# S5 stage: three real products per complex product in the table fills, two more doublings on GpSimd, one fill and one state product moved ahead

## Chip, core and metric

The kernel runs on 1 core of one Trainium2 chip. The metric is the device time of one execution in microseconds, the median of several runs. Engines: TensorE (PE in the profile), VectorE (DVE), ScalarE (ACT), GpSimd (POOL) and the SyncE queue that starts the weight loads (SP).

## What is computed

A trunk of four layers over 256 tokens of width 1024. Each layer is a token mixer and a gated MLP, each behind an RMS norm. The mixer of layer 0 and 3 is sparse attention, of layer 1 RWKV-7, of layer 2 the S5 state space layer that the change is about:

```python
def s5_mixer(h, a_re, a_im, log_step, b_re, b_im, c_re, c_im, d_skip, w_glu, b_glu):
    step = jnp.exp(log_step.astype(f32))[:, None]
    lam = lax.complex(a_re, a_im)
    lam_bar = jnp.exp(lam * step)
    b_bar = ((lam_bar - 1.0) / lam)[..., None] * lax.complex(b_re, b_im)
    c = lax.complex(c_re, c_im)
    u = h as (256 tokens, 64 groups, 16 channels)
    bu = einsum('gpc,sbgc->sbgp', b_bar, u)          # 64 complex states per group
    states: x[t] = lam_bar * x[t-1] + bu[t]          # associative scan
    y = real(einsum('gcp,sbgp->sbgc', c, states)) + d_skip * h
    y = gelu(y); z1, z2 = split(y @ w_glu + b_glu)
    return z1 * sigmoid(z2)
```

## The kernel before

Each engine has its own program, written out by hand and ordered by semaphores. The weights of the MLP and of the GLU come in tiles of 1 MB. Each is split into a high and a low part: ScalarE rounds (L395, `w_high`), VectorE subtracts for half 0 of the tile and GpSimd for half 1 (L403, `w_low`), and TensorE multiplies with both parts (L420 to L422; in the down projection L788 and L790). Two tiles are held split at a time, so a split can begin when the tile two before it is used up.

The S5 mixer works in chunks of 8 steps. Its tables depend on the parameters alone, and are built while TensorE does the down projection of layer 1. `s5_tables(dve, part)` is called once behind each of the first `LAST_PART` = 11 of the twelve tiles of that projection, in `add_down`. Parts 5 to 7 build `coef`, the factors of the complex products. Part 8 begins a table of powers, `grid`, and doubles it from 1 to 4 entries; parts 9 and 10 double it to 8 and 16 on VectorE (`double(4)`, `double(8)`, L2591 to L2627). The last doubling, to 32 entries, is GpSimd's (`last_doubling`, L2333), and needs the end of part 10. The part numbers count 3 * m + g, and the last weight split of the projection is that of part 9's place; it stands in front of `double(4)`, and the addition of the last sums to `xT` (L639, `x_ready`) stands behind `double(8)`.

Then come eight fills. Fill f = 2q + lag writes one of two tables, FB (lag 0) or GC (lag 1), for quarter q. VectorE makes the four real products of a complex product, 128x1024 each (`products`, L2715), from the raw parameters and from factors that `coefs` copied to PSUM (L2724); GpSimd joins them pairwise in two additions (`s5_pool`, L2344, `fill_added`). Fill 0 is made before the norm of the layer (L514, L517), since it needs no activations. VectorE's order after the norm is fill 1, fill 2, turn and scan of states 0, fill 3, fill 4, turn and scan 1, fills 5 to 7, turn and scan 2, turn and scan 3. `turned_in(q)` and `scan(q)` (L2749 to L2775) need the products of TensorE's `states(q)` (L2514, `v_full`).

TensorE turns the activations (L2464, L2472), then works through, in order: turned tables 0 (L2487), states 0, lag table 0 (L2501), turned 1, states 1, lag 1, turned 2, lag 2, states 2, lag 3, turned 3, lag 4, states 3, lag 5, 6, 7, and at last `from_states` (L2539) and `from_inputs` (L2525). Turned tables q need fill 2q, lag tables 2q and 2q + 1 need fill 2q + 1. Lag tables 1 to 5 share banks, so each of them, and table 7, waits until ScalarE has masked the one before (L2389, 8 instructions). `from_states` needs the fourth scan (`x_state`).

Of the kernel before, what the change touches and what calls it, by code (L numbers as in the profile page):

```python
# [35 lines left out]
HALF = 64  # L36
# [152 lines left out]
def trunk(nc, A, out, layers=(0, 1, 2, 3)):  # L189
    plan = make_plan(layers)  # L190
    ctx = ExitStack()
    with ctx:
# [28 lines left out]
        half_pi = sb("half_pi", 1)  # L221
        eps = sb("eps", 3)
# [32 lines left out]
        def wait_full(eng, key, more=0):  # L255
# [8 lines left out]
                         q_scale=2, v_ready=4, qi_ready=2, ki_raw=3, ki_root=1, ki_ready=1,  # L264
# [581 lines left out]
        def mlp_pool(pool, L):  # L846
# [300 lines left out]
        def dsa_act(act, L):  # L1147
# [91 lines left out]
            act.activation(ki_rs, ki_sum, ACT.Sqrt, bias=eps[:, 0:1], scale=1.0 / HALF).then_inc(sem("ki_root"), 1)  # L1239
# [59 lines left out]
        def dsa_dve(dve, L):  # L1299
# [92 lines left out]
            dve.wait_ge(sem("ki_root"), 1 + since("ki_root", L))  # L1392
# [870 lines left out]
        coef = work[:, 14, 0:1024].rearrange("p (v k g) -> p v k g", v=4, k=S5_L)  # L2263
        grid_tmp = work[:, 14, 1024:1536]
# [17 lines left out]
        FB_RE, FB_IM, GC_RE, GC_IM = range(4)  # L2282
        S5_DMAS = (6, 4, 4)
        LAST_PART = 11
# [5 lines left out]
        near_coef = banks[6].rearrange("p (b v k g) -> p b v k g", b=2, v=4, k=S5_L)  # L2290
        turned_a, turned_b = (banks[i].rearrange("p (r z) -> p r z", r=2) for i in (2, 3))
        second_terms = [[work[:, s, a:a + 1024] for s, a in pair] for pair in (((14, 1024), (8, 1024)), ((18, 0), (18, 1024)))]
# [29 lines left out]
        def last_doubling(pool):  # L2322

            pool.wait_ge(sem("angles_ready"), 3)
            have = S5_N // 2
            factor = [small(x).unsqueeze(2).to_broadcast([P, S5_H, have]) for x in (L8_RE, L8_IM)]
            x = [x[:, :, 0:have] for x in grid]
            t = grid_tmp[:, 0:S5_H * have].rearrange("p (g n) -> p g n", n=have)
            for half in range(2):
                dst = grid[half][:, :, have:S5_N]  # L2330
                for out_, a, b, op in ((t, x[1], factor[1 - half], ALU.mult), (dst, x[0], factor[half], ALU.mult),
                                       (dst, dst, t, (ALU.subtract, ALU.add)[half])):
                    pool.wait_ge(pool_step.sem, pool_step.mark(pool.tensor_tensor(out_, a, b, op)))  # L2333
# [121 lines left out]
        def s5_pe(pe, L):  # L2455
# [102 lines left out]
            turned_tables(3)  # L2558
            lag_tables(4)
            states(3)  # L2560
# [46 lines left out]
        def s5_tables(dve, part):  # L2607
# [4 lines left out]
            def double(have):  # L2612
# [9 lines left out]
                if 2 * have < S5_N:  # L2622
                    tt(small(TMP), small(L8_IM), small(L8_IM), ALU.mult)
                    tt(small(TURNS), small(L8_RE), small(L8_RE), ALU.mult)
                    then(dve.scalar_tensor_tensor(out=small(L8_IM), in0=small(L8_RE), scalar=2.0, in1=small(L8_IM),
                                                  op0=ALU.mult, op1=ALU.mult))
                    ins = dve.tensor_tensor(small(L8_RE), small(TURNS), small(TMP), ALU.subtract)  # L2627
                    if 4 * have == S5_N:
                        ins.then_inc(sem("angles_ready"), 1)
                    else:  # L2630
                        then(ins)
# [42 lines left out]
            if part == 5:  # L2674
# [4 lines left out]
                then(dve.scalar_tensor_tensor(out=coef[:, GC_IM], in0=table(MAG_P, S5_L), scalar=-1.0, in1=table(U_IM, S5_L),  # L2679
# [490 lines left out]
```

## Time and profile before

| | |
|---|---|
| median of 3 runs | 1466.46 us (1465.0 to 1473.16) |
| profiled execution | 1465.52 us, its span 1463.8 us |
| mean granted TensorE clock | 0.991 of full |
| busy | PE 95%, DVE 70%, ACT 55%, POOL 43% |
| S5 tables on VectorE | 740.6 to 799.2 us of the span |
| S5 from its first product to the GLU | 800 to 885 us of the span |

The span is what the profiler saw between first and last instruction. A median over runs and the one profiled execution need not agree; steps below are read from the profiled one. The idle time of an engine counts only where the engine after it waits.

### The profile page before, as it was taken

What the parts mean: (1) busy time and instruction counts of PE and PEld (TensorE: products, weight loads), DVE (VectorE), ACT (ScalarE), POOL (GpSimd) and SP (SyncE); (2) the same over time, 40 slices, a digit from 0 to 9 for tenths busy, and PEclk for the clock granted to TensorE, in tenths of its full rate; (3) what the DMA queues carried; (4) which work ended last, traced back from release to release, by engine and by line L of the source; (5) the groups of instructions that cost most, each with busy time, mean ns of one, the idle gap of its engine ahead of it and who ended that gap; (6) DMA issues with size and microseconds to landing.
All of it is one profiled execution on the core that took longest, in us unless ns stands there. A gap on an engine that the chain in (4) does not pass through costs nothing.

```text
span 1463.8 us, 33117 instructions
## 1 busy us (share of the span) xinstructions
PE 1395.5 (95%) x13742; PEld 1315.6 (90%) x13742; DVE 1029.0 (70%) x1656; ACT 801.4 (55%) x1332; POOL 630.3 (43%) x341
## 2 busy tenths in 40 slices
PE   7999999999999888999999679999999999999998
PEld 7999999989887777999989579999989998999988
DVE  7675888733595555897779895888754776788842
ACT  5576666534651334665653346576654468576542
POOL 3343365541005202495554653365553332355553
PEclk9999999999999999999999889999999999999999
DMA  5643565562443001475554004555555552455553
GB/s 170 197 132 100 165 195 188 168 201 93 144 144 116 4 4 60 144 225 179 176 177 138 1 2 145 173 175 193 173 187 157 162 167 94 149 190 180 179 175 107
DMA packets 207895, 209.59 MB, mean 143 GB/s; under 512 B 7938, under 2 KB 206898, under 8 KB 207762
## 3 DMA queue, kind: packets, MB, share of 16 engines
q1 hardware_dynamic: 206624, 206.12, 43.7%
q0 software_dynamic: 800, 1.46, 0.6%
q8 instruction: 99, 1.62, 0.5%
q14 instruction: 34, 0.28, 0.1%
q10 hardware_dynamic: 338, 0.10, 0.0%
HBM read 206.62 MB, written 1.05 MB: 142 GB/s over the span
## 4 chain that ended last, share of the span: by engine, by line
PE 79%; DVE 13%; ACT 4%; issue 2%; DMA 0%; POOL 0%; ACTq 0%; SPq 0%; DVEq 0%
PE psum L420 17%; PE psum L422 17%; PE psum L421 17%; PE psum L788 7%; PE psum L580 5%; PE psum L790 3%; DVE work L2591 2%; DVE x_low L532 2%; DVE work L2715 1%; ACT w_high L395 1%; DVE work L517 1%; DVE w_low L403 1%; PE psum L1719 1%; PE psum L1733 1%; PE psum L1051 1%
## 5 line engine op out<-in xcount | busy, mean ns | idle before, releaser
L403 POOL TENSOR_TENSOR w_low<-ring,w_high 128x1024 fp32r<-128x1024 f32 (+1 forms) x185 | 458.2, 2477 | 676.0 <-ACT w_high L395 675.9
L420 PE MATMUL psum<-x_high,w_high 128*128 128x256 f32 x1728 | 491.0, 284 | 3.5 <-DVE w_low L403 1.4
L395 ACT ACTIVATE w_high<-ring 128x1024 fp32r<-128x1024 f32 (+1 forms) x368 | 376.4, 1037 | 213.8 <-PE psum L422 122.0
L422 PE MATMUL psum<-x_high,w_low 128*128 128x256 f32 x1728 | 489.0, 283 | 0.0
L421 PE MATMUL psum<-x_low,w_high 128*128 128x256 f32 x1728 | 488.9, 283 | 0.0
L403 DVE TENSOR_TENSOR w_low<-ring,w_high 128x1024 fp32r<-128x1024 f32 x183 | 295.2, 1613 | 172.9 <-ACT w_high L395 171.6
L420 PEld LDWEIGHTS psum<-x_high,w_high 128*128 128x128 f32 x1728 | 331.6, 192 | 5.9 <-issue 3.1
L421 PEld LDWEIGHTS psum<-x_low,w_high 128*128 128x128 f32 x1728 | 331.7, 192 | 0.0
L422 PEld LDWEIGHTS psum<-x_high,w_low 128*128 128x128 f32 x1728 | 331.6, 192 | 0.0
L788 PE MATMUL psum<-inner,w_high 128*128 128x512 f32 x528 | 187.0, 399 | 1.4 <-DVE w_low L403 1.4
L899 DVE SCALAR_TENSOR_TENSOR work<-psum,par,work 128x255 f32<-128x255 f32 (+1 forms) x352 | 144.6, 472 | 46.5 <-ACT work L820 46.3
L820 ACT ACTIVATE work<-psum,par 128x256 f32<-128x256 f32 x176 | 89.1, 559 | 131.3 <-PE psum L422 131.3
L790 PE MATMUL psum<-inner,w_low 128*128 128x256 f32 x528 | 148.1, 281 | 0.0
L788 PEld LDWEIGHTS psum<-inner,w_high 128*128 128x128 f32 x528 | 99.2, 188 | 26.6 <-DVE w_low L403 1.3
L790 PEld LDWEIGHTS psum<-inner,w_low 128*128 128x128 f32 x528 | 99.7, 189 | 0.0
L908 DVE TENSOR_TENSOR work<-work 128x512 f32<-128x512 f32 x44 | 81.2, 1844 | 6.9 <-DVE work L899 5.0
L580 PE MATMUL psum<-work,ring 128*128 128x256 f32 x384 | 84.2, 379 | 0.9 <-issue 0.9
L580 PEld LDWEIGHTS psum<-work,ring 128*128 128x128 f32 x384 | 72.8, 190 | 12.5 <-issue 2.9
L420 PE MATMUL psum<-w_high,x_high 128*128 128x256 f32 x256 | 75.2, 294 | 0.0
L849 POOL TENSOR_TENSOR inner<-work,inner 128x512 f32 (+1 forms) x44 | 74.7, 1702 | 0.0
L422 PE MATMUL psum<-w_high,x_low 128*128 128x256 f32 x256 | 72.4, 283 | 0.0
L421 PE MATMUL psum<-w_low,x_high 128*128 128x256 f32 x256 | 72.4, 283 | 0.0
(332 smaller groups left out, 2226.1 us busy)
## 6 DMA issues: line engine op xcount, KB each, us to landing
ring<-in_ffn_w_up_dram SPq DMA_DIRECT2D x88, 1024.0 KB, 5.1
ring<-in_ffn_w_down_dram SPq DMA_DIRECT2D x32, 1024.0 KB, 5.0
ring<-in_dsa_w_in_dram SPq DMA_DIRECT2D x28, 1024.0 KB, 5.3
ring<-in_ffn_w_down_dram SPq DMA_DIRECT2D x16, 768.0 KB, 4.3
ring<-in_rwkv_w_rkv_dram SPq DMA_DIRECT2D x12, 1024.0 KB, 5.0
ring<-in_dsa_w_out_dram SPq DMA_DIRECT2D x8, 1024.0 KB, 5.0
ring<-in_s_w_glu_dram SPq DMA_DIRECT2D x8, 1024.0 KB, 5.4
ring<-in_rwkv_w_out_dram SPq DMA_DIRECT2D x4, 1024.0 KB, 5.0
```

What stands on the lines that cost most here:

```text
L395: act.activation(high, raw, ACT.Copy).then_inc(sem("w_rounded", b), 1)
L403: eng.tensor_tensor(low, raw, high.bitcast(F32), ALU.subtract).then_inc(sem("w_split", b), 1)
L420: pe.matmul(out_, lhs[0], rhs[0], start=start, stop=False, skip_group_check=True)
L421: pe.matmul(out_, lhs[0], rhs[1], start=False, stop=False, skip_group_check=True)
L422: return pe.matmul(out_, lhs[1], rhs[0], start=False, stop=stop, skip_group_check=True)
L580: mm = pe.matmul(out_, parts[b][:, k, b * P:(b + 1) * P], x[:, k, :], start=start, stop=stop, skip_group_check=True)
L788: pe.matmul(banks[bank][:, :], high[:, k, :], inner[:, :, c, :], start=first, stop=False, skip_group_check=True)
L790: mm = pe.matmul(banks[bank][:, 0:T], low[:, k, :], inner_high[:, c, :], start=False, stop=last, skip_group_check=True)
L820: act.activation(conv[:, j % 3, h, b, :], bank_of(key)[:, b * T:(b + 1) * T], ACT.Identity, bias=col("ffn_conv_b", c + L * 2 * FC, r), sca ...
L849: pool.tensor_tensor(inner_low[:, at(2 * j, r), :], gated[:, j % 3], inner_high[:, at(2 * j, r), :].bitcast(F32), ALU.subtract).then_inc(s ...
L899: dve.scalar_tensor_tensor(out=row, in0=bank[:, b * T:(b + 1) * T - lag], scalar=col("ffn_conv_w", c + (L * 3 + tap) * 2 * FC, r), in1=row ...
L908: dve.tensor_tensor(gated[:, j % 3], conv[:, j % 3, 0], conv[:, j % 3, 1], ALU.mult).then_inc(sem("gated_done"), 1)
```

## The change

1. A complex product is made from three real products: with B = b_re + i b_im and factor x + i y, the fill takes (b_re + b_im) * x once, b_im * (x + y), and b_re * (y - x), and then one subtraction and one addition. So VectorE makes 3 products of 128x1024 per fill instead of 4; GpSimd still makes 2 additions. The sums of the raw parameters (`b_sum`, `c_difference`, new tiles of 128x512) are two new GpSimd instructions; VectorE's first product of fills 0 and 1 waits for them. The table of factors `coef` grows from four to six blocks, which costs two more instructions of 128x256 in part 5 and two in part 7, and makes the copy to PSUM 128x384; the copy is no longer double buffered.
2. `double(4)` and `double(8)` move from VectorE to GpSimd, behind GpSimd's last weight splits of the down projection. They wait for the end of part 8 on VectorE. Each has 6 instructions over the table and 5 over 128x32.
3. Fill 3 is made before turn 0 on VectorE, instead of behind scan 0.
4. `states(3)` comes before `lag_tables(4)` on TensorE.
5. In the attention layers the semaphore `ki_root` is folded into `ki_raw`; the same instruction counts up, and the same one waits.

```diff
         def mlp_pool(pool, L):
             for m in range(4):
                 for g in range(3):
                     ahead(rest_of_weights, pool, (L, "down", m, g), 1)
+                    if before_s5(L) and m == 3 and g < 2:
+                        doubling(pool, 4 * (g + 1))
...
-        LAST_PART = 11
+        LAST_PART = 9
...
+        def s5_raw_sums(pool):
+
+            pool.wait_ge(sem("s5_in", 2), 16 * S5_DMAS[2])
+            pool.tensor_tensor(b_sum[:, :, :], b_raw[:, 0], b_raw[:, 1], ALU.add).then_inc(sem("raw_sums"), 1)
+            pool.wait_ge(sem("c_ready"), 2)
+            pool.tensor_tensor(c_difference[:, :, :], c_raw[:, 0], c_raw[:, 1], ALU.subtract).then_inc(sem("raw_sums"), 1)
 
         def s5_pool(pool, L):
 
+            s5_raw_sums(pool)
             for f in range(FILLS):
                 q, lag = divmod(f, 2)
                 if f == 0:
-                    last_doubling(pool)
+                    doubling(pool, S5_N // 2)
                 for v in range(2):
                     out_ = (FB, GC)[lag][:, q, v].rearrange("p g z -> p (g z)")
-                    pool.wait_ge(sem("fill_products"), 4 * f + 2 * v + 2)
-                    pool.tensor_tensor(out_, out_, second_terms[1 - f % 2][v],
-                                       ALU.add if v != lag else ALU.subtract).then_inc(sem("fill_added"), 1)
+                    pool.wait_ge(sem("fill_products"), 3 * f + v + 2)
+                    pool.tensor_tensor(out_, shared_terms[f % 2], out_,
+                                       ALU.subtract if v == lag == 0 else ALU.add).then_inc(sem("fill_added"), 1)
...
+            states(3)
             lag_tables(4)
-            states(3)
...
         def products(dve, f):
-            if f == 1:
-                dve.wait_ge(sem("fill_added"), 1)
-            if f >= 2:
+            if f < 2:
+                dve.wait_ge(sem("raw_sums"), f + 1)
+            else:
                 dve.wait_ge(sem("fill_added"), 2 * (f - 1))
-            for out_, a, b in ((outs[0], re, x), (terms[0], im, y), (outs[1], re, y), (terms[1], im, x)):
-                dve.tensor_tensor(out_, a, b, ALU.mult).then_inc(sem("fill_products"), 1)
+            for out_, x, y in ((shared, both, real), (outs[0], im, total), (outs[1], re, difference)):
+                dve.tensor_tensor(out_, x, y, ALU.mult).then_inc(sem("fill_products"), 1)
...
             products(dve, 1)
             coefs(dve, 1)
             products(dve, 2)
+            products(dve, 3)
             turned_in(0)
             scan(0)
-            products(dve, 3)
             coefs(dve, 2)
             products(dve, 4)
```

Line numbers of the changed kernel are higher by a few; L2591 there is L2612, L2715 is L2739, L403 is L405. VectorE around the end of the projection, before: the last weight split (`w_low_53`), the two doublings, the last addition to `xT`, the copy of the factors and fill 0.

```order
L403 TENSOR_TENSOR w_low_53<-ring,w_high_51 128x768
L2591 TENSOR_TENSOR work<-work 128x128
L2591 TENSOR_TENSOR work<-work 128x32x4 x2
...
L2591 TENSOR_TENSOR work<-work 128x256
L2591 TENSOR_TENSOR work<-work 128x32x8 x2
...
L639 TENSOR_TENSOR xT<-xT,psum 128x512
L2724 COPY psum<-work 128x256
L2715 TENSOR_TENSOR work<-work,psum 128x1024 x4
L514 RECIPROCAL psum<-rstd 128x256
```

The same place now:

```order
L405 TENSOR_TENSOR w_low_53<-ring,w_high_51 128x768
L641 TENSOR_TENSOR xT<-xT,psum 128x512
L2748 COPY psum<-work 128x384
L2739 TENSOR_TENSOR work<-b_sum,psum 128x1024
L2739 TENSOR_TENSOR work<-work,psum 128x1024 x2
L516 RECIPROCAL psum<-rstd 128x256
```

Both doublings are gone from between the split and the addition, and fill 0 reads `b_sum`, which GpSimd writes. GpSimd at the same place now, from its last weight split of the projection (before, L2333 followed the split at once):

```order
L405 TENSOR_TENSOR w_low_53<-ring,w_high_51 128x768
L2338 TENSOR_TENSOR work<-work 128x128
...
L2338 TENSOR_TENSOR work<-work 128x256
...
L2351 TENSOR_TENSOR b_sum<-work 128x512
L2353 TENSOR_TENSOR c_difference<-work 128x512
L2338 TENSOR_TENSOR work<-work 128x512
```

The two raw sums stand behind 22 instructions of the two doublings and ahead of the last doubling. TensorE at turned tables 3, before (L2487 turned tables, L2501 lag tables, L2514 states):

```order
L2487 MATMUL psum<-ident,work 128x128 x16
L2501 MATMUL psum<-work 128x128 x16
L2514 MATMUL psum<-work 64x32 x32
L2501 MATMUL psum<-work 128x128 x48
```

And now (L2508, L2535, L2522 are the same three):

```order
L2508 MATMUL psum<-ident,work 128x128 x16
L2535 MATMUL psum<-work 64x32 x32
L2522 MATMUL psum<-work 128x128 x64
```

The states moved ahead of the first of the four remaining lag tables.

## Rows read from the trace of the kernel before

**Rows 1.** The page, section 4: shares of the chain that ended last, by engine.

```profile
PE 79%; DVE 13%; ACT 4%; issue 2%; DMA 0%; POOL 0%; ACTq 0%; SPq 0%; DVEq 0%
```

**Rows 2.** Chain that ended last, in order of time, 700 to 960 us: start, us, what.

```profile
800.13 4.62 DVE work L2715 x4
851.82 4.68 POOL work L2344 x2
856.54 3.77 PE psum L2487 x16
860.31 2.58 PE psum L2501 x32
871.52 3.68 PE psum L2539 x247
```

**Rows 3.** Timeline of PE: start, us, instruction, [idle before it <-what ended it].

```profile
792.82 0.39 PE L420 MATMUL psum<-inner,w_high 128*128 128x256 f32 x1 [1.28 <-DVE w_low L403]
797.23 2.56 PE L503 MATMUL psum<-ident 128*128 128x128 f32 x22
815.90 1.09 PE L2487 MATMUL psum<-ident,work 128*128 128x128 f32 x8 [2.11 <-ACT work L2399]
831.84 2.06 PE L2514 MATMUL psum<-work 128*64 128x32 f32 x64 [0.69 <-ACT work L2405]
```

**Rows 4.** Timeline of DVE, columns as in rows 3.

```profile
770.35 0.42 DVE L2591 TENSOR_TENSOR work<-work 128x256 f32<-128x256 f32 x1
770.81 0.42 DVE L2679 SCALAR_TENSOR_TENSOR work<-work 128x256 f32<-128x256 f32 x1
790.26 0.19 DVE L2627 TENSOR_TENSOR work<-work 128x32 f32<-128x32 f32 x1
792.68 2.37 DVE L2591 TENSOR_TENSOR work<-work 128x128 f32<-128x128 f32 x8
799.08 0.68 DVE L639 TENSOR_TENSOR xT<-xT,psum 128x512 f32<-128x512 f32 x1
804.67 1.75 DVE L514 RECIPROCAL psum<-rstd 128x256 f32<-128x256 f32 x1
823.58 0.69 DVE L2749 TENSOR_TENSOR work<-psum,work 128x512 f32<-128x512 f32 x1 [4.38 <-PE psum L2514]
829.24 4.61 DVE L2715 TENSOR_TENSOR work<-work,psum 128x1024 f32<-128x1024 f32 x4
838.75 0.68 DVE L2749 TENSOR_TENSOR work<-psum,work 128x512 f32<-128x512 f32 x1
```

**Rows 5.** Line L2591 on DVE from 776.5 to 781 us: min/median/max ns.

```profile
L2591 DVE TENSOR_TENSOR work<-work x4: 418/424/2645, 776.7 to 780.3; 128x256 f32<-128x256 f32 x4
```

**Rows 6.** Timeline of POOL, columns as in rows 3.

```profile
771.06 1.90 POOL L403 TENSOR_TENSOR w_low<-ring,w_high 128x768 fp32r<-128x768 f32 x1 [3.95 <-ACT w_high L395]
777.05 2.43 POOL L403 TENSOR_TENSOR w_low<-ring,w_high 128x1024 fp32r<-128x1024 f32 x1 [4.09 <-ACT w_high L395]
799.24 7.17 POOL L2333 TENSOR_TENSOR work<-work 128x512 f32<-128x512 f32 x6 [10.56 <-DVE work L2627]
```

**Rows 7.** POOL and DVE groups by form: xcount | busy us, mean ns.

```profile
L2333 POOL TENSOR_TENSOR work<-work 128x512 f32<-128x512 f32 x6 | 6.8, 1130 | 11.0 <-DVE work L2627 10.6
L2029 POOL TENSOR_SCALAR work<-work,par 128x256 f32<-128x256 f32 x8 | 8.0, 1009 | 0.1
L2949 POOL TENSOR_TENSOR centre_head<-ident,mean_head 128x128 f32<-128x128 f32 x1 | 0.5, 513 | 0.1
L2934 POOL MEMSET blocks<- 64x32 f32 x6 | 0.8, 134 | 0.2
```

**Rows 8.** Timeline of ACT: the root of the norm, and a copy of turned tables.

```profile
803.28 0.47 ACT L508 ACTIVATE rstd<-psum,eps 128x256 f32<-128x256 f32 x1 [2.86 <-PE psum L496]
860.35 0.60 ACT L2405 ACTIVATE work<-psum 128x512 f32<-128x512 f32 x1 [0.26 <-PE psum L2487]
```

**Rows 9.** Busy time by stretch: us, PE (x) PEld (x) DVE (x) ACT (x) POOL (x), clock, DMA.

```profile
800.00:885.00 85.00, 63.03 (x1278) 56.75 (x1276) 72.39 (x101) 37.00 (x86) 48.30 (x24) 0.88 0.04 12
```

More of the change, by code:

```diff
@@ L221, in trunk @@
         half_pi = sb("half_pi", 1)
+        b_sum = sb("b_sum", S5_H, S5_C)
+        c_difference = sb("c_difference", S5_H, S5_C)
         eps = sb("eps", 3)
@@ L1391, in dsa_dve @@
             split("i", 1)
-            dve.wait_ge(sem("ki_root"), 1 + since("ki_root", L))
+            dve.wait_ge(sem("ki_raw"), 4 + since("ki_raw", L))
             then(dve.reciprocal(ki_rs, ki_rs))
@@ L2289, in trunk @@
         YT_BANKS = ((0, 1, 4, 5), (2, 3, 6, 7))
-        near_coef = banks[6].rearrange("p (b v k g) -> p b v k g", b=2, v=4, k=S5_L)
+        near_coef = banks[6][:, 0:6 * S5_L * S5_Q].rearrange("p (v k g) -> p v k g", v=6, k=S5_L)
         turned_a, turned_b = (banks[i].rearrange("p (r z) -> p r z", r=2) for i in (2, 3))
-        second_terms = [[work[:, s, a:a + 1024] for s, a in pair] for pair in (((14, 1024), (8, 1024)), ((18, 0), (18, 1024)))]
+        shared_terms = [work[:, 18, a:a + 1024] for a in (0, 1024)]
         FILLS = 8
@@ L2320, in s5_load, with doubling, then @@
                         pool.dma_start(b_raw[r, v], A[f"s5_b_{name}"][0, g].rearrange("g p c -> p g c")).then_inc(sem("s5_in", 2), 16)
-        def last_doubling(pool):
-            pool.wait_ge(sem("angles_ready"), 3)
-            have = S5_N // 2
+        def doubling(pool, have):
+            def then(ins):
+                pool.wait_ge(pool_step.sem, pool_step.mark(ins))
+            if have == 4:
+                pool.wait_ge(sem("angles_ready"), 3)
             factor = [small(x).unsqueeze(2).to_broadcast([P, S5_H, have]) for x in (L8_RE, L8_IM)]
@@ L2329, in last_doubling @@
             for half in range(2):
[L2330 to L2333, printed above, removed]
+                dst = grid[half][:, :, have:2 * have]
+                then(pool.tensor_tensor(t, x[1], factor[1 - half], ALU.mult))
+                then(pool.tensor_tensor(dst, x[0], factor[half], ALU.mult))
+                then(pool.tensor_tensor(dst, dst, t, (ALU.subtract, ALU.add)[half]))
+            if 2 * have < S5_N:
+                then(pool.tensor_tensor(small(TMP), small(L8_IM), small(L8_IM), ALU.mult))
+                then(pool.tensor_tensor(small(TURNS), small(L8_RE), small(L8_RE), ALU.mult))
+                then(pool.tensor_tensor(small(L8_IM), small(L8_RE), small(L8_IM), ALU.mult))
+                then(pool.tensor_tensor(small(L8_IM), small(L8_IM), small(L8_IM), ALU.add))
+                then(pool.tensor_tensor(small(L8_RE), small(TURNS), small(TMP), ALU.subtract))
+        def s5_raw_sums(pool):
[3 more added lines that the diff above has]
+            pool.tensor_tensor(c_difference[:, :, :], c_raw[:, 0], c_raw[:, 1], ALU.subtract).then_inc(sem("raw_sums"), 1)
         def s5_pool(pool, L):
+            s5_raw_sums(pool)
             for f in range(FILLS):
@@ L2621, in double @@
                     tt(dst, dst, t, (ALU.subtract, ALU.add)[half])
[L2622 to L2631, printed above, removed]
+                tt(small(TMP), small(L8_IM), small(L8_IM), ALU.mult)
+                tt(small(TURNS), small(L8_RE), small(L8_RE), ALU.mult)
+                then(dve.scalar_tensor_tensor(out=small(L8_IM), in0=small(L8_RE), scalar=2.0, in1=small(L8_IM),
+                                              op0=ALU.mult, op1=ALU.mult))
+                ins = dve.tensor_tensor(small(L8_RE), small(TURNS), small(TMP), ALU.subtract)
+                if have == 2:
+                    ins.then_inc(sem("angles_ready"), 1)
+                else:
+                    then(ins)
             if part == 0:
@@ L2689, in s5_tables @@
                 tt(dst, dst, table(MAG_N, S5_L), ALU.mult)
+                if part == 7:
+                    tt(coef[:, FB_SUM], coef[:, FB_RE], dst, ALU.add)
+                    tt(dst, dst, coef[:, FB_RE], ALU.subtract)
             if part == 8:
@@ L2695, in s5_tables @@
                 double(2)
-            if part >= 9:
-                double(2 ** (part - 7))
         def products(dve, f):
```

34 lines of the change are left out of this document (19 added, 15 removed).

## Prediction

> **What bounds the kernel now.** I read the page first. Four fifths of the chain that ended last is TensorE, 13% is VectorE [rows 1], and the whole of the change lies in a short part of the span, so I asked for that chain in order of time from 700 to 960 us. Between the MLP of layer 1 and the GLU it is hardly TensorE's: fill 0 on VectorE, later two additions on GpSimd, then turned tables 3, lag table 4 and in the end `from_states` at 871.52 [rows 2]. VectorE is busy 72.39 of the 85 us there, GpSimd 48.30, TensorE 63.03 [rows 9]. So what counts is which engine is late at each handover, and I take three stretches apart.
>
> First, the end of the down projection. TensorE waits 1.28 us for the last weight split of VectorE and then runs through, and its first idle turn behind the projection starts at 797.23, so the projection ends about then [rows 3]. VectorE adds the last sums only at 799.08, for it is still in `double(4)` and `double(8)` [rows 4]: 1.8 us late.
>
> Second, from there to turned tables 0 at 815.90 [rows 3]. Fill 0 starts at 800.13 [rows 2], the reciprocal at 804.67 [rows 4], and the root that it needs ended at 803.28 + 0.47 = 803.75 [rows 8]. So fill 0, not the root, holds the norm, by 0.9 us. From the reciprocal to turned tables 0 it is 11.2 us of work that the change leaves alone.
>
> Third, from turned tables 0 to `from_states`, 871.52 - 815.90 = 55.6 us.
>
> **The change, part by part.**
>
> *Tables on VectorE.* Parts 5 and 7 get two instructions of 128x256 each. From one such start to the next it is 0.46 us [rows 4], so 4 x 0.46 = 1.84 us. They stand ahead of the last weight split, on which TensorE already waits; so they pass through to TensorE in full. There is a second cost. A VectorE instruction over `work` alone took 2645 ns where its median is 424 [rows 5], and just then GpSimd ran one subtraction of 2.43 us from 777.05 [rows 6]: VectorE stood still until GpSimd was done. The trace agrees with the Trainium skill (SBUF — State Buffer, "Who interferes with whom"): a VectorE instruction with two SBUF inputs and a GpSimd one that reads SBUF exclude each other for a whole instruction, while one with an operand in PSUM is not concerned. Before, part 5 just slipped past such a GpSimd instruction: it was through at 771.23, and GpSimd ran from 771.06 to 772.96 [rows 4, 6]. Now two more instructions of part 5 fall into it, up to 1.7 us of standing still, and splits that come later make TensorE late as well. Bounds for the end of part 8, now 790.45 [rows 4]: 1.84 us later at the least, 1.84 + 1.7 + 0.6 = 4.1 at the most (0.6 for one more instruction caught). I take 3.0, so 793.5.
>
> *The doublings that leave VectorE.* They took from 792.68 to 799.08, 6.4 us [rows 4], but behind the last split, in time in which TensorE had yet 4.4 us of matmuls. Their removal can give the 1.8 us of lateness at the addition and no more. The last split comes 3.0 us later plus up to 0.4 for a GpSimd instruction in its way, say 3.2; TensorE ends at 797.3 + 3.2 = 800.5, and the addition starts at 800.6 instead of 799.08. So this place loses 1.5 us instead of gaining. The root follows 4.67 us behind the addition, at 805.3, and fill 0 could start at 801.9 (1.05 as before, and 0.2 for the longer copy).
>
> *The doublings on GpSimd.* They start at 793.6, and fill 0 waits for `b_sum` behind them. The trace has no such small GpSimd instructions over `work`. Nearest rows: 128x512 in 1.13 us with 0.07 between two (6 in 7.17) [rows 6, 7], which for 128x256 is 0.57 and for 128x128 0.28 by size; above, a one-input 128x256 took 1.01, and a two-input 128x128 took 0.51 [rows 7]. For 128x32 the low end is a memset of 64x32, 0.13 [rows 7]; the high end is 0.07 by size and the 0.23 that the 0.51 row has over its own size, 0.30. With 0.07 to each, low: 6 x 0.35 + 6 x 0.64 + 10 x 0.20 = 7.9 us; high: 6 x 0.58 + 6 x 1.08 + 10 x 0.37 = 13.7. I take 9.0 (6 x 0.42 + 6 x 0.64 + 10 x 0.26), nearer the low end, since L2333 is the same operation on the same table. VectorE's last split holds GpSimd for another 0.95, and `b_sum` is 1.1. So `b_sum` is there at 793.6 + 9.0 + 0.95 + 1.1 = 804.65 (low, from 792.4, it is 802.3; high, from 794.7, it is 810.5).
>
> The Trainium skill (GPSIMD Engine Reference, "Engine selection") puts two-input elementwise work on VectorE, GpSimd being about twice as slow. Taken alone, that rule would have the two doublings cost twice VectorE's 6.4 us, 12.8 us, and `b_sum` come at 808.4; the row of L2333 gives 9.0, and the measured row is what the sum goes by.
>
> Fill 0 then has three products, 4.62 / 4 = 1.155 each, 3.5 us: 804.7 to 808.2. The reciprocal, which the root would allow at 805.3, starts at 808.2 instead of 804.67: **+3.5 us**. If GpSimd were early this would be 801.9 + 3.5, +0.7. Fill 0's additions are ready at 804.65 + 1.1 + 7.17 + 4.7 = 817.6, before turned tables 0 at 819.4, so they don't add.
>
> *Turned tables 0 to turned tables 3.* Call the start of turned tables 0 zero. Before, the product of states 1 was there at 831.84 + 2.06 - 815.90 = 18.0, but VectorE came to turn 1 at 838.75 [rows 3, 4], 22.85: it had fills 3 and 4 in front, four products each. Now fill 3 fits into VectorE's wait of 4.38 us for states 0 [rows 4]. From turn 0 (at 7.7) it is 5.66 us of turn and scan (823.58 to 829.24 [rows 4]), 0.6 for the copy, 3.5 for fill 4: 17.5, so turn 1 starts with TensorE's states at 18.0. Gain 4.8. Then turn and scan to 23.8, two products of fill 5 to 26.1, fills 5 and 6 on GpSimd at 4.68 each [rows 2] to 35.5. There turned tables 3 start; before it was 856.54 - 815.90 = 40.6. Gain **5.1 us**. The fourth product saved in fills 6 and 7 is worth nothing here: GpSimd's two additions, 4.7, are longer than three products, 3.5.
>
> *From turned tables 3 to `from_states`.* Before 871.52 - 856.54 = 15.0: turned tables, then lag tables 4, 5 and 7 with ScalarE's masks between. Now `states(3)` stands first. It waits for the last ScalarE copy (860.35 + 0.60 [rows 8] against 860.31 for the lag table [rows 2]), 0.65, and takes 2.06 as states 1 did [rows 3]; lag table 4 then takes 2.06 rather than 2.58, since TensorE has run for longer. That is +2.2. What it buys is an earlier scan 3: that one would end 6.6 + 5.7 = 12.3 us behind the start of turned tables 3, where `from_states` starts after 17.2. It is early for nobody. Cost **+2.2 us**, covered by nothing.
>
> *Rest.* The semaphore in the attention layers changes no instruction's neighbour: 0. The copy of factors now waits for VectorE's own products, about 0.1 us twice, in VectorE's slack.
>
> Sum: +3.5 - 5.1 + 2.2 = +0.6 us on the profiled execution, 1465.52 to 1466.1. That execution lies 0.94 below the median of the three runs, so the median becomes **1467.0 us**.
>
> **Rivals.** *VectorE was the limit all along* (faster). Then every instruction taken from it counts: 8 products, 9.2, and 6.4 of doublings, less 1.84 and 0.7 for longer copies: -13.1, 1453.4 us. For it: VectorE's 72.39 busy of 85 [rows 9]. Against: its wait of 4.38 for states 0, and the doublings lay behind the last split. 0.05.
>
> *GpSimd quick, the moved states free*: `b_sum` not waited for and no extra collision, start shift 0, and -5.1: 1461.4 us. The lag tables would have to have slack of 2.2 us, but the chain runs through them to `from_states` [rows 2]. 0.10; it is within 0.5%.
>
> *GpSimd's hand-over is the new wait* (slower). The place is `b_sum`. Each microsecond that it comes later than 804.65 is one on the end; from 804.1 on the change loses. By my high bound, 810.5, it is +6.5: 1472.9 us. 0.18. To lose over 0.5% it has to come after 811.4, or 0.72 us for each of the 22 small instructions; with TensorE left idle from 806.5 to 811 and its granted clock low behind that (the stretch's mean is 0.88 of full [rows 9]), 1475 us. 0.06.
>
> **How the numbers follow.** 0.5% is 7.3 us, about what can be told from no change here. My forecast, within 3 us of before, has 0.61. Faster by over 0.5%: 0.05. Slower: 0.06. Within: 0.61 + 0.10 + 0.18 = 0.89. The range takes in the low bound, -2.9 with fill 0 hardly late, and the high one, +6.5, with 1.5 us more below, the distance of the median from the lowest of the three runs: 1462 to 1473 us.
>
> **What would show it.** VectorE's addition of the last sums at about 800.6, not before 799; fill 0 with a wait of 2 to 3 us for GpSimd's `b_sum`; the reciprocal near 808; turned tables 0 near 819.4; turn 1 right behind states 1 with no VectorE work in its way; turned tables 3 about 35.5 us behind turned tables 0; `from_states` 17 us behind that, with scan 3 done 4 to 5 us early. It is wrong if GpSimd's small instructions cost under 0.2 or over 0.6 us on average, if the last split meets the GpSimd subtractions in another order, or if TensorE's clock falls at another place.

## The result, and the profile after

The changed kernel takes 1475.67 us (median of 14 runs, 1469.52 to 1478.81), the kernel before 1469.18 us in the same comparison (14 runs). The ratio is 1.0046, 95% interval 1.0030 to 1.0061: slower by 4.4 to 9.0 us. In a later comparison (6 runs against 23) the same code gave 1.0074 (1.0052 to 1.0096). The profiled execution took 1474.58 us, 9.06 more than that of before.

Chain that ended last of the changed kernel, in order of time: start, us, what.

```profile
802.79 0.26 POOL work L2346
...
809.18 1.31 POOL b_sum L2351
810.62 3.48 DVE work L2739 x3
814.10 1.68 DVE psum L516
...
848.90 2.27 DVE work L2739 x2
851.24 9.34 POOL work L2365 x4
860.62 3.79 PE psum L2508 x16
...
865.08 2.06 PE psum L2535 x64
867.14 2.01 PE psum L2522 x32
869.17 2.18 ACT work L2410 x8
871.39 3.58 PE psum L2522 x32
```

Against [rows 2], GpSimd has taken VectorE's place ahead of fill 0, the fills up to turned tables 3 are shorter, and behind them the chain runs through TensorE and ScalarE by turns. The timelines of the changed kernel, TensorE first, then VectorE, GpSimd and ScalarE (start, us, instruction, [idle before it <-what ended it]):

```profile
800.18 0.58 PE L422 MATMUL psum<-inner,w_high 128*128 128x256 f32 x1 [2.96 <-DVE w_low L405]
...
807.27 2.56 PE L505 MATMUL psum<-ident 128*128 128x128 f32 x22
...
825.25 1.09 PE L2508 MATMUL psum<-ident,work 128*128 128x128 f32 x8 [2.11 <-ACT work L2420]
...
871.39 5.34 PE L2522 MATMUL psum<-work 64*128 64x128 f32 x64 [2.27 <-ACT work L2410]
877.22 2.06 PE L2522 MATMUL psum<-work 64*128 64x128 f32 x32 [0.49 <-ACT work L2410]
```

```profile
744.58 0.19 DVE L2612 TENSOR_TENSOR work<-work 128x32 f32<-128x32 f32 x1 [1.66 <-ACT work L2383]
...
775.28 2.02 DVE L2700 SCALAR_TENSOR_TENSOR work<-work 128x256 f32<-128x256 f32 x1
...
799.04 1.09 DVE L405 TENSOR_TENSOR w_low<-ring,w_high 128x768 fp32r<-128x768 f32 x1
807.54 0.69 DVE L641 TENSOR_TENSOR xT<-xT,psum 128x512 f32<-128x512 f32 x1 [7.41 <-PE psum L424]
...
810.62 1.22 DVE L2739 TENSOR_TENSOR work<-b_sum,psum 128x1024 f32<-128x1024 f32 x1 [1.92 <-POOL b_sum L2351]
```

```profile
797.88 0.41 POOL L2338 TENSOR_TENSOR work<-work 128x128 f32<-128x128 f32 x1 [3.78 <-DVE work L2647]
...
799.39 1.00 POOL L2338 TENSOR_TENSOR work<-work 128x128 f32<-128x128 f32 x1
...
801.50 0.24 POOL L2342 TENSOR_TENSOR work<-work 128x32 f32<-128x32 f32 x1
...
803.12 0.63 POOL L2338 TENSOR_TENSOR work<-work 128x256 f32<-128x256 f32 x1
```

```profile
813.33 0.47 ACT L510 ACTIVATE rstd<-psum,eps 128x256 f32<-128x256 f32 x1 [4.44 <-PE psum L498]
```

And the busy time of the changed kernel by stretch, around TensorE's wait for the last split and around its wait for the mask of lag table 4 (us, PE (x), PEld (x), DVE (x), ACT (x), POOL (x), clock, DMA, GB/s):

```profile
797.00:799.00 2.00, 0.22 (x2) 0.02 (x1) 1.86 (x6) 0.00 (x0) 0.96 (x3) 1.00 0.02 8
799.00:801.00 2.00, 0.82 (x4) 0.82 (x5) 1.13 (x2) 1.83 (x2) 1.77 (x4) 0.62 0.00 0
...
803.00:805.00 2.00, 2.00 (x11) 2.00 (x11) 0.00 (x0) 0.00 (x0) 1.76 (x4) 0.50 0.92 320
...
872.00:874.00 2.00, 2.00 (x22) 2.00 (x22) 0.86 (x3) 0.00 (x0) 0.00 (x0) 0.50 0.00 0
```

The clock is full in the first stretch and half within the second, before the wait is over at 800.18. From 803 to 805 TensorE is busy without a gap and yet does 11 matmuls in 2 us, at a clock of 0.50.

The first table instruction stands at 744.58 us, at 740.59 before: 4.0 us were gone ahead of anything that S5 does. So I count from there. In every kernel it is the first L2612 (L2591 before). "Turned 0" and "turned 3" are the starts of these tables on TensorE, "GLU" is TensorE's first matmul of it; all in us behind the first table instruction, each from one profiled execution.

| kernel | last addition | root done | reciprocal | turned 0 | turned 3 | `from_states` | GLU |
|---|---|---|---|---|---|---|---|
| before | 58.5 | 63.2 | 64.1 | 75.3 | 116.0 | 130.9 | 145.0 |
| changed | 63.0 | 69.2 | 69.4 | 80.7 | 116.0 | 134.6 | 148.7 |
| changed, again | 61.8 | 68.1 | 69.5 | 82.3 | 119.8 | 140.6 | 155.4 |
| layout_only | 58.5 | 63.2 | 64.1 | 75.4 | 114.8 | 129.7 | 144.1 |
| before_states_ahead | 58.6 | 63.3 | 64.2 | 75.5 | 116.1 | 137.3 | 151.3 |
| states_back | 61.7 | 68.0 | 69.4 | 80.7 | 116.6 | 131.0 | 145.3 |
| raw_early | 61.8 | 68.1 | 68.1 | 79.3 | 116.8 | 137.6 | 151.5 |
| factors_late | 56.9 | 63.1 | 66.3 | 78.8 | 112.1 | 132.9 | 147.0 |
| three_fixed | 57.0 | 63.2 | 63.2 | 74.5 | 109.7 | 124.2 | 138.5 |
| fixed_vector_doublings | 60.5 | 63.5 | 65.1 | 78.0 | 114.0 | 128.3 | 142.9 |
| fixed_states_ahead | 57.2 | 63.5 | 63.5 | 74.7 | 110.2 | 127.2 | 141.5 |
| fill3_back | 61.9 | 68.2 | 69.5 | 80.8 | 119.6 | 140.4 | 154.5 |
| fixed_fill3_back | 56.9 | 63.1 | 63.1 | 74.4 | 112.3 | 126.9 | 141.1 |

The two profiles of the changed kernel show how much of this table is one execution's and not the kernel's. Against before, turned tables 0 are 5.4 and 7.0 us later, the way from there to turned tables 3 is 5.3 and 3.1 us shorter (35.4 and 37.5 us for 40.6), and the way on to `from_states` is 3.7 and 5.9 us longer. In all, the S5 part is 3.7 us longer in the first and 10.3 in the second; the two ratios say 6.8 and 10.9 us (0.46% and 0.74% of some 1470). What lies ahead of the tables and behind S5 is the next question.

### The profile page after: what moved, and what is told of

Read it like the earlier page. It is cut to its first block, busy times and chain, and to the rows that moved or that the text cites. A ratio compares the mean times of both kernels' runs of the same rounds, so it can differ in the third digit from the quotient of the medians.

```text
span 1472.8 us, 33118 instructions
## 1 busy us (share of the span) xinstructions
PE 1403.3 (95%) x13742; PEld 1322.6 (90%) x13742; DVE 1018.9 (69%) x1632; ACT 801.0 (54%) x1332; POOL 641.0 (44%) x365
## 3 DMA queue, kind: packets, MB, share of 16 engines
HBM read 206.62 MB, written 1.05 MB: 141 GB/s over the span
## 4 chain that ended last, share of the span: by engine, by line
PE 80%; DVE 11%; ACT 5%; issue 2%; POOL 1%; DMA 0%; ACTq 0%; SPq 0%; DVEq 0%; POOLq 0%
PE psum L422 17%; PE psum L424 16%; PE psum L423 16%; PE psum L790 7%; PE psum L582 5%; PE psum L792 3%; DVE work L2612 2%; DVE x_low L534 2%; ACT w_high L397 1%; DVE work L519 1%; DVE w_low L405 1%; PE psum L1723 1%; PE psum L1737 1%; PE psum L1055 1%; PE psum L2522 1%
## 5 line engine op out<-in xcount | busy, mean ns | idle before, releaser
L405 POOL TENSOR_TENSOR w_low<-ring,w_high 128x1024 fp32r<-128x1024 f32 (+1 forms) x185 | 457.1, 2472 | 687.5 <-ACT w_high L397 687.5
L405 DVE TENSOR_TENSOR w_low<-ring,w_high 128x1024 fp32r<-128x1024 f32 x183 | 297.2, 1624 | 173.0 <-ACT w_high L397 171.6
L422 PE MATMUL psum<-w_high,x_high 128*128 128x256 f32 x256 | 75.3, 294 | 0.0
L851 POOL TENSOR_TENSOR inner<-work,inner 128x512 f32 (+1 forms) x44 | 74.7, 1701 | 0.0
```

Of the source, the lines that this page charges most:

```text
L405: eng.tensor_tensor(low, raw, high.bitcast(F32), ALU.subtract).then_inc(sem("w_split", b), 1)
L422: pe.matmul(out_, lhs[0], rhs[0], start=start, stop=False, skip_group_check=True)
L851: pool.tensor_tensor(inner_low[:, at(2 * j, r), :], gated[:, j % 3], inner_high[:, at(2 * j, r), :].bitcast(F32), ALU.subtract).then_inc(s ...
```

## Experiments

A ratio below is always to the kernel before, timed beside it. The kernels were timed in groups: the first four together, without the changed kernel; then three_fixed, fixed_vector_doublings and fill3_back, with the changed kernel once more; then the last three. A difference of two ratios out of different groups is weaker than one inside a group: the changed kernel itself gave 1.0046 and 1.0074. "Below the changed kernel's" means below 1.0046 where nothing else is said, and each interval is some 0.0013 to 0.0022 wide to either side.

### Chance ahead of the tables, or the layout

Edit to the kernel before:

```diff
+        b_sum = sb("b_sum", S5_H, S5_C)
+        c_difference = sb("c_difference", S5_H, S5_C)
...
-scale=1.0 / HALF).then_inc(sem("ki_root"), 1)
+scale=1.0 / HALF).then_inc(sem("ki_raw"), 1)
...
-            dve.wait_ge(sem("ki_root"), 1 + since("ki_root", L))
+            dve.wait_ge(sem("ki_raw"), 4 + since("ki_raw", L))
```

> The kernel before with only the two new tiles of 128x512 allocated (unused) and the attention semaphore folded; all S5 work as before. Of the changed kernel's 9.0 us more in the profiled execution, 4.0 lie ahead of the S5 tables (VectorE's first table instruction 744.58 instead of 740.59 us) and 1.4 behind S5. Theory A: that part is chance between executions, from where TensorE's granted clock dips, and not from the edits: ratio 0.999 to 1.001 to the kernel before. Theory B: the shifted memory layout or the semaphore costs 3 to 5 us: ratio 1.002 to 1.0035.

Ratio 1.0003 (0.9988 to 1.0019). Theory A. In the thirteen profiles of the table the first table instruction lies between 740.0 (three_fixed) and 748.4 us (fixed_vector_doublings), with the same work ahead of it but for the layout and one semaphore. So the 4.0 us say nothing of the change, and ahead of the landmark one profile against one is good to no better than some 8 us.

### The raw sums made early

Edit to the changed kernel, in `mlp_pool` and at the head of `s5_pool`:

```diff
+                    if before_s5(L) and (m, g) == (0, 1):
+                        s5_raw_sums(pool)
...
-            s5_raw_sums(pool)
```

> The changed kernel with GpSimd's b_sum and c_difference made early in the down projection (behind its second weight split there, while VectorE waits), so that fill 0 no longer waits for them. Theory A (my prediction's): GpSimd's hand-over holds the norm; fill 0 then starts 1.9 us earlier and so do the reciprocal and turned tables 0: ratio lower than the changed kernel's by about 0.001. Theory B: the root of the norm came equally late (it ended at 813.80, the reciprocal started at 814.02), because TensorE ended the projection late; then fill 0 starts at 808.8 in place of 810.6 but the reciprocal moves by less than 0.3 us and the time not at all. I hold with B.

Ratio 1.0020 (1.0005 to 1.0034), 0.0026 below the changed kernel's. In its profile the root is done 68.1 behind the first table instruction and the reciprocal starts at 68.1, so the norm now hangs on the root, and the reciprocal is 1.4 us earlier, not the 0.3 at most that B says: in the changed kernel's second profile root and reciprocal lie 68.1 and 69.5, and only in its first did they meet. So `b_sum` held the norm by 0.2 to 1.4 us. Both theories are off in size, since the root, which was to be at 64.7, is at 68 to 69: two lates side by side, and taking one away shows little of either. The intervals of the two ratios overlap (from 1.0030, up to 1.0034), so the size of the 0.0026 is open; the S5 part in the one profile, 151.5, lies between the changed kernel's two, 148.7 and 155.4.

### States 3 behind lag tables 4 again

Edit to the changed kernel:

```diff
-            states(3)
             lag_tables(4)
+            states(3)
             lag_tables(5)
```

> The changed kernel with states(3) behind lag_tables(4) again, as before the change. Theory A: moving it ahead only lengthened the chain of lag tables: from turned tables 3 to from_states 18.6 us become 15 to 16, the time falls by 2.2 to 3.6 us (ratio lower by 0.0015 to 0.0025 than the changed kernel's). Theory B: scan 3 is what from_states waits for, and the move was worth its place: the distance stays or grows, time the same or up to 2 us more.

Ratio 1.0013 (0.9996 to 1.0030), 0.0033 or 4.8 us below the changed kernel's. From turned tables 3 to `from_states` it is 14.4 us instead of 18.6, and 20.8 in the changed kernel's second profile. Theory A, and more than its sum; but here too the intervals touch (1.0030).

### The four factor instructions behind the last split

Edit to the changed kernel:

```diff
-        LAST_PART = 9
+        LAST_PART = 10
...
-                tt(table(GROW, S5_L), table(MAG_P, S5_L), table(U_IM, S5_L), ALU.mult)
-                then(dve.scalar_tensor_tensor(out=coef[:, GC_DIFF], in0=table(GROW, S5_L), scalar=-1.0, in1=coef[:, GC_RE],
-                                              op0=ALU.mult, op1=ALU.subtract))
-                tt(coef[:, GC_SUM], coef[:, GC_RE], table(GROW, S5_L), ALU.subtract)
+                then(dve.scalar_tensor_tensor(out=coef[:, GC_DIFF], in0=table(MAG_P, S5_L), scalar=-1.0, in1=table(U_IM, S5_L),
+                                              op0=ALU.mult, op1=ALU.mult))
...
-                if part == 7:
-                    tt(coef[:, FB_SUM], coef[:, FB_RE], dst, ALU.add)
-                    tt(dst, dst, coef[:, FB_RE], ALU.subtract)
+            if part == 9:
+                for total, difference, real in ((FB_SUM, FB_DIFF, FB_RE), (GC_SUM, GC_DIFF, GC_RE)):
+                    tt(coef[:, total], coef[:, real], coef[:, difference], ALU.add)
+                    tt(coef[:, difference], coef[:, difference], coef[:, real], ALU.subtract)
```

> The changed kernel with the four additional factor instructions of 128x256 moved from parts 5 and 7 to behind VectorE's last weight split of the down projection, where VectorE waits. Theory A: those four, with the GpSimd instruction that one of them fell into, make VectorE's last split late, TensorE waits 2.96 us for it, its granted clock halves behind the wait and the last 6 rows of the projection take 7.3 us instead of 4.4. Then here the wait is 0.5 to 1.5 us, the clock stays, the last addition comes 4 to 6 us earlier, but fill 0 still waits for b_sum: the reciprocal 2 to 3 us earlier, time down 2 to 3 us. Theory B: the wait comes from elsewhere (ScalarE, weight loads): the addition stays where it was, time the same within 1 us.

Ratio 1.0040 (1.0025 to 1.0055). The wait and the addition are as A has them: TensorE waits 1.01 us for the last split instead of 2.96, and the last addition comes 6.1 us earlier (56.9 against 63.0). TensorE's timeline:

```profile
797.70 0.39 PE L422 MATMUL psum<-inner,w_high 128*128 128x256 f32 x1 [1.01 <-DVE w_low L405]
```

The reciprocal is 3.1 us earlier (66.3), as the table has it, but turned tables 0 only 1.9, and no gain clear of the noise reaches the end: 0.0006, where A had 2 to 3 us. Fill 0 waits 4.87 us for `b_sum`, TensorE stands idle in the meantime, and its granted clock is at half from 69 to 72 us behind the first table instruction, where the activations are to be turned. So the wait has moved to a later place, and in this profile a fall of the clock stands behind it there. Turned tables 3 to `from_states` took 20.8 us, 2.2 more than in the changed kernel's first profile, which takes back over half of the 3.9 us that turned tables 3 had gained.

### All three repairs together

three_fixed is the changed kernel with the three edits above at once.

> The changed kernel with all three repairs: raw sums made early, the four factor instructions behind the last weight split, states(3) behind lag_tables(4). Theory A (my sum, as corrected by the traces): the last addition is 1.6 us earlier than in the kernel before, the reciprocal follows the root (about 63 us behind the first table instruction, before 64.1), turned tables 0 to 3 take 35.4 instead of 40.6, and from_states follows 15 to 16 behind: S5 stage 5 to 6 us shorter than before, ratio 0.996 to 0.997. Theory B: the repairs overlap (each removes a wait that another then holds) or the clock dips move: ratio 0.998 to 1.001.

And the changed kernel once more, on the same chip:

> The changed kernel once more, on the chip of the three others of this call. Theory A: its loss is real and between 0.3% and 0.6%: ratio 1.003 to 1.006. Theory B: most of the 0.46% was chance of where TensorE's clock dips: ratio 1.001 to 1.003. By its S5 stage alone (3.7 us more than before in the first profile) it should be 1.0025.

three_fixed: 0.9953 (0.9935 to 0.9971), 1461.93 us against 1469.15. The changed kernel: 1.0074. The changed kernel comes out slower than either theory of its second timing had it; three_fixed is a little faster than A's, and its S5 part is 6.5 us shorter than before (138.5 for 145.0), where A said 5 to 6. So three of the four ideas, with the fourth (states 3 ahead) taken back and two groups of instructions in other places, are 0.5% faster than before, where the change as made is 0.5 to 0.7% slower. That the three together turn the loss into a gain is shown; two of them do it already (fixed_states_ahead below). Whether they help or hinder each other is not: to the changed kernel's 1.0046 they bring 0.0026, 0.0033 and 0.0006 apart and 0.0093 together, but to its 1.0074 it is 0.0054, 0.0061 and 0.0034 apart, 0.0149 in sum, and 0.0121 together. The first reading says more than the sum, the second less. Timeline of VectorE in three_fixed:

```profile
796.95 0.69 DVE L641 TENSOR_TENSOR xT<-xT,psum 128x512 f32<-128x512 f32 x1 [2.60 <-PE psum L424]
...
798.15 1.22 DVE L2739 TENSOR_TENSOR work<-b_sum,psum 128x1024 f32<-128x1024 f32 x1
799.28 2.34 DVE L2739 TENSOR_TENSOR work<-work,psum 128x1024 f32<-128x1024 f32 x2
803.22 1.76 DVE L516 RECIPROCAL psum<-rstd 128x256 f32<-128x256 f32 x1 [1.59 <-ACT rstd L510]
```

VectorE now waits for TensorE at the addition and for the root at the reciprocal, and for GpSimd at neither. And TensorE behind turned tables 3:

```profile
849.65 3.77 PE L2509 MATMUL psum<-ident,work 128*128 128x128 f32 x16 [5.31 <-POOL work L2366]
853.35 2.22 PE L2523 MATMUL psum<-work 64*128 64x128 f32 x32
855.50 2.06 PE L2536 MATMUL psum<-work 128*64 128x32 f32 x64
857.84 3.84 PE L2523 MATMUL psum<-work 64*128 64x128 f32 x64 [0.29 <-ACT work L2411]
862.17 2.06 PE L2523 MATMUL psum<-work 64*128 64x128 f32 x32 [0.48 <-ACT work L2411]
```

States 3 (855.50) fills the time in which ScalarE masks lag table 4; the two waits that are left are 0.29 and 0.48 us.

### Each part on the repaired kernel

From three_fixed to fixed_vector_doublings:

```diff
-                    if before_s5(L) and m == 3 and g < 2:
-                        doubling(pool, 4 * (g + 1))
...
-        LAST_PART = 10
+        LAST_PART = 11
...
+            if part >= 9:
+                double(2 ** (part - 7))
```

> three_fixed with double(4) and double(8) on VectorE again, behind its last weight split. Theory A: the doublings on VectorE lie behind the end of the projection: four factor instructions and two doublings, 8.2 us, against 4.4 to 6 us of matmuls; the last addition comes at 60.5 behind the first table instruction, the reciprocal at 65 to 66, so 2 to 3 us slower than three_fixed, ratio higher by 0.0015 to 0.002. Theory B: the place of the doublings is worth nothing, same ratio within 0.001.

0.9993 (0.9980 to 1.0007): 0.0040 slower than three_fixed. Theory A in place (addition 60.5, reciprocal 65.1), twice its size in time. The reciprocal is 1.9 us later than in three_fixed, and turned tables 0 follow it by 12.9 us instead of 11.2: the clock is at half there, as in factors_late. By turned tables 0 it is 3.5 us.

From the changed kernel to fill3_back, and from three_fixed to fixed_fill3_back:

```diff
-            products(dve, 3)
             turned_in(0)
             scan(0)
+            products(dve, 3)
```

> The changed kernel with fill 3 behind scan 0 again. Theory A: the gain of 5.1 us from turned tables 0 to turned tables 3 comes mostly from fill 3 standing in VectorE's wait; without it 3.5 us come back between turn 0 and turn 1, turned tables 3 stand 37.5 to 38.5 us behind turned tables 0 instead of 35.4, ratio higher than the changed kernel's by 0.0015 to 0.0025. Theory B: turn 0 starts earlier without fill 3 in front (it waits for GpSimd in the changed kernel), and the sum is the same within 1 us.

> three_fixed with fill 3 behind scan 0 again. Theory A: as in the changed kernel, where it made no difference (1.0078 against 1.0074), VectorE reaches turn 1 later by up to 3.5 us, turned tables 3 come 1 to 3 us later: ratio 0.996 to 0.9975. Theory B: TensorE's states(1) or GpSimd's additions hold turn 1 anyway: 0.995 to 0.996.

In the changed kernel 1.0078 (1.0056 to 1.0100), not to be told from the 1.0074 beside it: B by the time. By the profile it is nearer A: turned tables 3 stand 38.8 us behind turned tables 0, where the changed kernel has 35.4 and 37.5. In the repaired one 0.9973 (0.9960 to 0.9986), 0.0020 slower than three_fixed (0.9935 to 0.9971), with turned tables 3 at 112.3 instead of 109.7: A's place and size, though the intervals overlap. Whether the same edit is worth more in the repaired kernel than in the changed one, these intervals can't tell.

From the kernel before to before_states_ahead, and from three_fixed to fixed_states_ahead:

```diff
+            states(3)
             lag_tables(4)
-            states(3)
             lag_tables(5)
```

> The kernel before with one part of the change alone: states(3) ahead of lag_tables(4). Theory A: it lengthens the chain from turned tables 3 to from_states from 15.0 to 18 or 21 us, since TensorE then waits twice for ScalarE's masks with nothing in between, and its clock falls in these waits: ratio 1.002 to 1.004. Theory B (my prediction's size): 2.2 us, ratio 1.0015. Theory C: scan 3 ends earlier and from_states with it, ratio under 1.

> three_fixed with states(3) ahead of lag_tables(4) again, so raw sums early and factors late alone repaired. Theory A: the move costs 4 to 6 us here as well, and the two other repairs bring 4 to 6 together (apart they brought 0.0026 and 0.0006 or less, since each left the other's wait): ratio 0.998 to 1.0. Theory B: the move costs only in the company of the late start: ratio 0.9955 to 0.9975.

Alone on the kernel before: 1.0039 (1.0020 to 1.0058), 5.7 us; at the upper end of A, and over twice the prediction's 2.2, from which the interval (2.9 to 8.5 us) keeps clear. On the repaired kernel: 0.9974 (0.9959 to 0.9989), 0.0021 or 3.1 us above three_fixed, with overlapping intervals again, and with 17.1 us from turned tables 3 to `from_states` against 14.5. That is +2.6, close to the 2.2 of my sum. The ratio is B's, but B's reason is not: before_states_ahead has no late start either and pays 6.4. Why the one is 2.6 and the other 6.4 (21.3 against 14.9) shows in TensorE's timeline of before_states_ahead, which is to be read beside [rows 2]:

```profile
858.50 3.77 PE L2487 MATMUL psum<-ident,work 128*128 128x128 f32 x16 [5.41 <-POOL work L2344]
862.95 3.63 PE L2514 MATMUL psum<-work 128*64 128x32 f32 x64 [0.69 <-ACT work L2405]
866.51 3.79 PE L2501 MATMUL psum<-work 64*128 64x128 f32 x32
872.57 7.26 PE L2501 MATMUL psum<-work 64*128 64x128 f32 x96 [2.27 <-ACT work L2389]
```

and in its busy time by stretch (us, PE (x), PEld (x), DVE (x), ACT (x), POOL (x), clock, DMA, GB/s):

```profile
864.00:866.00 2.00, 2.00 (x44) 2.00 (x41) 1.93 (x4) 0.00 (x0) 1.42 (x1) 0.50 0.04 8
866.00:868.00 2.00, 2.00 (x26) 1.94 (x26) 1.47 (x4) 0.00 (x0) 0.00 (x0) 0.50 0.00 0
...
872.00:874.00 2.00, 1.43 (x22) 1.43 (x24) 0.37 (x1) 0.52 (x2) 0.00 (x0) 0.90 0.00 0
874.00:876.00 2.00, 2.00 (x22) 2.00 (x22) 0.00 (x0) 0.52 (x3) 0.00 (x0) 0.50 0.00 0
```

The 64 matmuls of states 3 took 3.63 us and the 32 of lag table 4 3.79, both at a clock of 0.50 (1.2 GHz), where three_fixed ran 2.06 and 2.22. The clock was half already at the turned tables; in the kernel before, it rose again while turned tables and lag table 4 ran without a gap (lag table 4 took 2.58 us there, [rows 2]). Then comes a wait of 2.27 us for ScalarE's mask, which states 3 used to fill, and the clock falls once more (0.50 from 874). The same stretch of fixed_states_ahead, timeline and clock:

```profile
855.70 3.73 PE L2509 MATMUL psum<-ident,work 128*128 128x128 f32 x16 [5.30 <-POOL work L2366]
860.11 2.06 PE L2536 MATMUL psum<-work 128*64 128x32 f32 x64 [0.69 <-ACT work L2427]
862.10 2.06 PE L2523 MATMUL psum<-work 64*128 64x128 f32 x32
866.43 3.84 PE L2523 MATMUL psum<-work 64*128 64x128 f32 x64 [2.28 <-ACT work L2411]
```

```profile
865.52:867.52 2.00, 1.09 (x18) 1.09 (x20) 1.92 (x4) 0.86 (x4) 0.00 (x0) 1.00 0.00 0
867.52:869.52 2.00, 2.00 (x40) 2.00 (x38) 0.42 (x1) 0.99 (x4) 0.00 (x0) 1.00 0.00 0
```

The same order, the same waits (0.69 and 2.28 us), and a full clock from states 3 on. So the wait for the mask is already in the 2.6 us: it takes the place of the time that states 3 had filled, and is not paid on top. The other 4.2 us (21.3 against 17.1) are the clock's. Lag table 5 begins 14.1 us behind turned tables 3 instead of 10.7, which is 3.3 us from states 3 and lag table 4 at half clock, ahead of the wait; the last 0.9 lies behind it.

## Why the prediction was wrong

Forecast: +0.6 us, 1467.0, range 1462 to 1473. Measured: 1475.67, and +6.8 by the ratio. Of the 8.7 us between the two times, 2.7 are the kernel before, 1469.18 in this comparison and not 1466.46. The engines and most waits were as forecast. Two terms of the sum were too small, `b_sum` by its own cost, and both by TensorE's clock, which the sum left out.

**Right.** The four factor instructions made the last split late, one fell into a GpSimd subtraction (775.28, 2.02 us for an instruction of 0.42, with GpSimd running from 775.15), and part 8 ended 53.2 us behind the first table instruction; my 793.5 is 52.9. The rule of the Trainium skill (SBUF — State Buffer, "Who interferes with whom") holds the other way round too: GpSimd's 128x128 doubling step took 1.00 instead of 0.41 us at 799.39, while VectorE's last split of 1.09 ran from 799.04. Fill 0 waited for `b_sum`, 1.92 us and 3.10 in the second profile; I had said 2 to 3. From turned tables 0 to 3 it took 35.4 us, by my sum 35.5; that the two agree so well is in part luck, since the second profile has 37.5. Scan 3 was early for nobody: its last instruction was over at 872.93, `from_states` began at 879.21.

**"Cost +2.2 us"** for states 3 ahead of lag table 4 is the step that failed most. It was 3.7 and 5.9 us in the two profiles of the changed kernel (18.6 and 20.8 for 14.9), 6.4 in before_states_ahead, and 5.7 us alone by its ratio. The order of events was right, and so was the size while the clock held: 2.6 in fixed_states_ahead, where the granted clock was full behind turned tables 3. What I left out is the clock. In the changed kernel's first profile the 64 matmuls behind the wait of 2.27 us took 5.34 us (871.39; three_fixed's row 857.84 has 3.84), 1.5 us more. In its second profile, as in before_states_ahead, states 3 and lag table 4 ran at half clock too (3.63 us at 866.08, 3.76 at 869.64), which is the larger part of the 5.9. That the wait brings the fall about is what the profiles suggest, and not shown: a further fall of the clock in or behind the wait shows in six of the seven profiles with states 3 ahead and in none of the six others, but in fixed_states_ahead the same wait of 2.28 us did not halve it.

**"+3.5 us"** for the start of turned tables 0 was 5.4 and 7.0. One part is a mis-sized term: the two doublings took from 797.88 to 809.18, 11.3 us, where I had 9.0 and 0.95. The ten instructions of 128x32 were 0.24 each, not 0.19, and those of 128x128 0.41 to 0.46. That is +1.4, and 1.30 instead of 1.1 for `b_sum`; it comes at 65.9, forecast 64.1. These 1.9 us are all that is missing in the first profile. The further 1.6 of the second lie between the reciprocal and turned tables 0, 12.9 us for the 11.2 that I had as work left alone: the granted clock was at half there from about 815 to 818.6.

Beside it stands an error that cost nothing in these two profiles: the root, which I had at 64.7 with 3 us to spare, was done at 69.2 and 68.1, nearly as late as fill 0. "The root follows 4.67 us behind the addition" hung it on the wrong row. It follows TensorE's end of the projection, whose idle turns and norm matmuls run on by themselves: 6.5 us before (797.23 to 803.75) and 6.5 now (807.27 to 813.80); only because the addition was late were there 4.67 between it and the root. By that alone it would be 66.4. And "TensorE ends at 797.3 + 3.2" had the wait for the split in it, 1.28 before and 2.96 now, but TensorE going on at full clock. It ran the last tile in part or mostly at half: 7.1 us (800.18 to 807.27) for the 4.4 of before, and 5.9 in each of the four other profiles with this wait. raw_early and factors_late show the two lates apart: each removes one and leaves the other.

**The rival that came true** is the slower one, in place (`b_sum`), not in size: its price of 6.5 us has `b_sum` 5.9 us later than forecast, and it was 1.9. That 6.5 lies so near the 6.8 measured is luck. What filled the gap was the clock, which I had put at the far end of that rival with 0.06 instead of into the forecast. The rows of before had it: mean granted clock 0.88 in that stretch. I took that as a given of the stage and not as a price that added waits can raise. The low end of the range had a slip of its own: with `b_sum` at its low bound, 802.3, the start moves by 1.1 us, so the sum there is -1.8 and not -2.9.

**"Their removal can give the 1.8 us"** and no more holds at the addition: three_fixed has it 1.5 us earlier than before. It does not bound the time. In the repaired kernel, doublings on GpSimd instead of VectorE are worth 0.40%, 5.9 us: 3.5 at the addition (the factor instructions stand behind the split there too), 1.9 at the reciprocal, 3.5 again at turned tables 0, since the clock stayed full on the way in three_fixed and was at half in fixed_vector_doublings.

Open stays what sets off a fall of the clock, how much each repair is worth by itself, and what the three real products are worth: no run has them without the rest, or the rest without them.

## What to carry to other kernels

Before pricing a moved piece of work, ask what it filled, and at which clock the matmuls behind it will run. States 3 covered a wait for ScalarE. Taken out of it, it cost 2.6 us where the clock stayed full and 3.7 to 6.4 where it did not, so a sum at full clock is the least price and not the middle one. Where two engines hand over at about the same time, take both lates away in one build before judging: taking away `b_sum`'s or the split's alone showed little here. When many small instructions go to GpSimd, price each from its own size, since small ones do not cost in proportion, and put what another engine waits for ahead of them. And profile a kernel twice before reading microseconds out of one profile.

## What the runs showed of the hardware

- TensorE's granted clock fell to 0.50 in or just behind waits of 2.3 to 3 us in the changed kernel (2.96 at 800.18, 2.27 at 871.39). At the first it did so in all five profiles that have it, and the last tile then took 5.9 us in four of them and 7.1 in one, for 4.4 at full clock. Behind the 1.28 us of [rows 3] and 1.01 in factors_late it did not fall at that place. In the second stretch it did not always fall (fixed_states_ahead).
- A GpSimd subtraction, multiplication or addition of 128x32 took 0.24 us, 128x128 0.41, 128x256 0.63, 128x512 1.05 (1.30 for `b_sum`): at the small end a quarter of the size costs over half of the time. VectorE took 0.19 for 128x32 and 0.42 for 128x256.
- Executions of one kernel in one comparison differ by 9 to 12 us (1463.52 to 1473.99 and 1464.08 to 1476.13 for the kernel before), while the landmarks ahead of the tables in single profiles spread over 8.4 us. Differences under 0.3% between two profiles need a landmark near the change, and a ratio of many runs.
